# GpSimd makes the weights' low parts in pieces of at most 256 columns in place of 384 to 1280

## What is computed

```
for l in range(2):
    mod, modc = silu(c) @ w_mod[l] + b_mod[l], silu(c_ctx) @ w_mod[l] + b_mod[l]   # 6 x 1024 each
    h, hc = modulated rms_norm of x and xc
    p, pc = h @ w_in[l], hc @ w_in[l]
    y_a = chunked mLSTM (both directions), y_b = latent attention, y_c = neighbourhood attention
    y = (sigmoid(gates) * (y_a, y_b, y_c) summed) @ w_out[l]
    x = x + g1 * y
    x = x + g2 * (square(relu(norm(x) @ w_ff1[l])) @ w_ff2[l])
    # the same for the context stream xc, in the first layer alone
```

## Time and profile before

| what | value |
|---|---|
| median of 3 runs | 1687.56 us (1683.96 to 1689.25) |
| the profiled execution's own time | 1691.04 us |
| its span, first to last instruction | 1689.3 us |
| mean granted clock of PE | 0.97 of full speed |
| PE busy | 93% of the span |
| DVE, ACT, POOL busy | 59%, 45%, 41% |
| PE's share of the chain of waits | 77% |

### The profile page before, as it was taken

How to read it: one execution, slowest core, us unless ns; L and a number is a source line. 1 busy time by engine, 2 the same in 40 slices (tenths; PEclk the granted TensorE clock), 3 DMA queues, 4 the chain that set the end, 5 groups by cost and what they waited for, 6 DMA issues and landing times.

```text
span 1689.3 us, 24992 instructions
## 1 busy us (share of the span) xinstructions
PE 1576.3 (93%) x9728; PEld 1341.6 (79%) x9728; DVE 1000.5 (59%) x1737; ACT 757.5 (45%) x1506; POOL 691.4 (41%) x407
## 2 busy tenths in 40 slices
PE   7897998989999999899999998979898989989998
PEld 3776778967877687688888886967897876889998
DVE  5755934875367762668696964144127287665554
ACT  4424653455544643523232334347436545554443
POOL 0451324634343012455554543534455453234442
PEclk9998999999999999999999998989999999999999
DMA  8442434421225132243455742132520343435553
GB/s 328 185 183 81 181 113 150 151 100 53 83 100 193 26 128 97 75 159 122 169 199 193 279 151 100 69 100 81 162 101 26 122 144 101 157 129 192 179 178 122
DMA packets 69852, 230.64 MB, mean 137 GB/s; under 512 B 18280, under 2 KB 24808, under 8 KB 56424
## 3 DMA queue, kind: packets, MB, share of 16 engines
q1 hardware_dynamic: 60880, 213.67, 35.7%
q10 hardware_dynamic: 8856, 15.39, 2.5%
HBM read 216.45 MB, written 12.58 MB: 136 GB/s over the span
## 4 chain that ended last, share of the span: by engine, by line
PE 77%; DVE 9%; ACT 6%; POOL 4%; issue 3%; DMA 1%; ACTq 0%; DVEq 0%
PE bank L1843 39%; PE bank L1925 10%; PE bank L1881 8%; PE bank L1863 4%; PE bank L1907 3%; PE bank L2228 2%; PE bank L2204 2%; PE bank L2215 2%; POOL wL L693 1%; ACT wH L832 1%; POOL wL L695 1%; PE bank L2078 1%; DVE arena L1339 1%; DVE mjunk L1268 1%; PE bank L1946 1%
## 5 line engine op out<-in xcount | busy, mean ns | idle before, releaser
L695 POOL TENSOR_TENSOR wL<-raw,wH 128x768 fp32r<-128x768 f32 (+3 forms) x198 | 327.7, 1655 | 354.5 <-ACT wH L832 354.4
L832 ACT ACTIVATE wH<-raw 128x768 fp32r<-128x768 f32 (+6 forms) x396 | 296.9, 807 | 387.4 <-PE bank L1843 287.3
L693 POOL TENSOR_TENSOR wL<-raw,wH 128x1280 fp32r<-128x1280 f32 (+2 forms) x144 | 298.8, 2075 | 413.3 <-ACT wH L832 413.3
L1843 PE MATMUL bank<-hH,wH 128*128 128x512 f32 (+1 forms) x720 | 247.8, 344 | 2.4 <-POOL wL L695 1.5
L1843 PE MATMUL bank<-hH,wL 128*128 128x512 f32 (+1 forms) x720 | 244.6, 340 | 0.0
L1843 PE MATMUL bank<-hL,wH 128*128 128x512 f32 (+1 forms) x720 | 244.5, 340 | 0.0
L1843 PE MATMUL bank<-oH,wH 128*128 128x512 f32 (+1 forms) x576 | 194.5, 338 | 0.5 <-issue 0.5
L1843 PE MATMUL bank<-oH,wL 128*128 128x512 f32 (+1 forms) x576 | 193.6, 336 | 0.0
L1843 PE MATMUL bank<-oL,wH 128*128 128x512 f32 (+1 forms) x576 | 193.6, 336 | 0.0
L1271 DVE SCALAR_TENSOR_TENSOR acc<-acc,cb 128x1024 f32<-128x1024 f32 x88 | 167.2, 1914 | 2.5
L1881 PE MATMUL bank<-hH,wH 128*128 128x512 f32 (+1 forms) x384 | 138.8, 362 | 18.0 <-POOL wL L695 11.7
(11 more groups left out here) (213 smaller groups left out, 3140.7 us busy)
## 6 DMA issues: line engine op xcount, KB each, us to landing
raw<-in_p_ff SPq DMA_DIRECT2D x64, 1024.0 KB, 4.8
acc<-in_p_mod SPq DMA_DIRECT2D x44, 1024.0 KB, 5.4
raw<-in_p_ml SPq DMA_DIRECT2D x12, 1024.0 KB, 5.0
raw<-in_p_na SPq DMA_DIRECT2D x12, 1024.0 KB, 4.9
raw<-in_p_mgc SPq DMA_DIRECT2D x16, 512.0 KB, 3.5
raw<-in_p_mga SPq DMA_DIRECT2D x16, 512.0 KB, 3.5
raw<-in_p_mgb SPq DMA_DIRECT2D x16, 512.0 KB, 3.6
raw<-in_p_out SPq DMA_DIRECT2D x8, 1024.0 KB, 4.8
```

The costliest lines, as they stand in the source:

```text
L693: pool.tensor_tensor(l_[:, 0:cut], r_[:, 0:cut], h_[:, 0:cut].bitcast(F32), ALU.subtract)
L695: pool.tensor_tensor(l_[:, cut:k * w], r_[:, cut:k * w], h_[:, cut:k * w].bitcast(F32), ALU.subtract)\
L832: act.activation(flat(wH, n)[:, part], flat(raw, n)[:, part], ACT.Copy)\
L1843: ins = pe.matmul(dst, w_[:, kk, c:c + P], r_[:, kk, lo:TOK], start=kk == k0 and m == 0, stop=kk == k0 + kn - 1 and m == 2)
```

## The change

In `low`, each of POOL's two subtractions is cut into instructions of at most 256 columns. The waits for `w_high` stay where they were, ahead of the first piece of each part, and `w_split` is raised by the last piece. What is computed is the same, and no other engine's list changes.

```diff
-                if not SHARED[n]:
-                    pool.wait_ge(*S("w_high").at(2 * n + 1))
-                    pool.tensor_tensor(l_[:, 0:cut], r_[:, 0:cut], h_[:, 0:cut].bitcast(F32), ALU.subtract)
-                pool.wait_ge(*S("w_high").at(2 * n + 2))
-                pool.tensor_tensor(l_[:, cut:k * w], r_[:, cut:k * w], h_[:, cut:k * w].bitcast(F32), ALU.subtract)\
-                    .then_inc(S("w_split").handle, 1)
+                for part, (lo, hi) in enumerate(((0, cut), (cut, k * w))):
+                    if part or not SHARED[n]:
+                        pool.wait_ge(*S("w_high").at(2 * n + 1 + part))
+                        for at in range(lo, hi, 256):
+                            cols_ = slice(at, min(at + 256, hi))
+                            ins = pool.tensor_tensor(l_[:, cols_], r_[:, cols_], h_[:, cols_].bitcast(F32), ALU.subtract)
+                ins.then_inc(S("w_split").handle, 1)
```

## The result

The changed kernel takes **1700.76 us** (median of 4 runs, 1699.39 to 1704.67), the kernel before 1687.05 in the same comparison: ratio 1.0087, 95% interval 1.0072 to 1.0103, so it is 13.7 us slower (12 to 17). The forecast was 1696 us, slower. The profiled execution took 1700.19 us with a span of 1698.5. The one on record for the kernel before (1691.04) is 4 us over its median; a second one, taken later (experiment e8), took 1688.35, and against that one the changed kernel is 11.84 us late. One execution of experiment e10 took 3371.54 us, twice all others, and is left out of e10's median.

What follows compares the result with a forecast made beforehand. PE was taken to bound the long feed-forward stretches, POOL counting only where PE waits for it. 6.6 + 5.5 - 3.6 = +8.5 us on the median 1687.56 gave 1696 us; own range 1690 to 1702, 8-in-10 range 1686 to 1709.

Steps and rivals of the forecast that it cites:

- Part one: At eleven places of POOL on the chain, 47 more instructions at 0.14 us each: 6.6 us lost.
- Part two: At 66.67, 151.31 and 701.05 us, DVE operations take more turns between POOL's pieces: 2.0, 2.0 and 1.5, sum 5.5 us lost.
- The rival that DVE keeps out: DVE gets no turn between pieces without a wait between them: +8 us, 1695.5 us; chance 0.12.
- The rival that the feed-forward of layer 0 tips over: POOL's blocks there end too late, PE waits in up to 13 at 0.7 us: +9 more, 1705 us; chance 0.14.
- In the feed-forward of layer 0 PE stays without gaps: Sign of the forecast in the profile after: no PE waits there, a block's pieces and three multiplies ending 0.5 us early.
- Part three: PE's waits for DVE at lines 1606 and 1656 shorten, 2 of 7.0 and 1.6 of 4.0 us: 3.6 us gained.
- Behind pieces of 0.69 or 0.42 us the seven take about 5: Step of Part three: DVE's seven operations, 466.21 to 473.63 us before, take about 5 us behind the shorter pieces.
- one per POOL instruction: Claim in Part three: line 1339's four small multiplies, 0.49 us alone, take 4.08 by entering singly behind POOL's instructions.
- two instructions and then free: Step of Part three: PE's longest wait for DVE, 2.2 us, gains almost nothing, as eight instructions will hold DVE instead.

Runs made afterwards that it cites:

- e8: The kernel before, unchanged, run once more for a second profiled execution: median 1686.23 us, profiled execution 1688.35 us.
- e10: The kernel before with pieces of at most 256 columns only for the latent attention weights of layer 0: 1685.17 us, ratio 0.9990.
- e1: The changed kernel with the feed-forward weights of layer 0 split whole again, one instruction per part: 1692.86 us, ratio to before 1.0035.
- e2: The kernel before with the feed-forward weights of layer 0 alone split in pieces of at most 256 columns: 1697.45 us, ratio 1.0061.
- e6: The changed kernel with the two multiplies of every modulation chunk on 128 of their 1024 columns: 1686.67 us, 8.3 us over e5.
- e5: The kernel before with the two multiplies of every modulation chunk on 128 of their 1024 columns: 1678.41 us, ratio 0.9955.

## Why the prediction was right, and where it was off

The sign held, and of the three parts the first two nearly to the size. The total was close because the other errors had opposite signs.

**Part one** (47 x 0.14 = 6.6 lost). The price stands at three sizes: 0.14 at 256 columns, 0.15 more per piece at 128, and at 512 a block of five takes 5.17 for 4.74, 0.14 again. The part had 27 of its 47 instructions between 1055 and 1277 us (three full blocks, one `gate`, one shared, four `ns`), 3.8 us. The same stretch of the program in the base, in the changed kernel and in e1, whose instructions there are those of the changed kernel: its length, then PE's busy time, and the granted clock third from the end.

```profile
1055.00:1277.00 222.00, 195.65 (x1481) 181.78 (x1481) 65.94 (x164) 103.03 (x218) 107.45 (x82) 0.95 0.32 103
```

```profile
1065.60:1292.80 227.20, 197.03 (x1482) 182.48 (x1481) 66.05 (x164) 102.88 (x218) 122.31 (x189) 0.93 0.31 100
```

```profile
1054.70:1285.10 230.40, 200.31 (x1482) 186.00 (x1481) 66.07 (x164) 102.88 (x217) 121.94 (x189) 0.92 0.30 99
```

PE is idle 26.35, 30.17 and 30.09 us: 3.8 and 3.7 more than in the base, as priced. The rest of the 5.2 and 8.4 us is busy time, 1.4 and 4.7 us longer at a lower granted clock. That is also why taking the feed-forward's pieces out (e1) gave back less than they cost alone (e2); what set the clock lower in e1 stays open. So price and count fit this stretch. Which places stand on the chain did change, as in these three `gate` blocks (seven waits at line 1926 for four):

```profile
1158.43 5.82 POOL wL L696 x10
...
1164.60 2.90 POOL wL L696 x5
```

**Part two** (5.5 lost by turns at three places). At the first place 1.98 us measured, 2.0 forecast. At the second POOL's five pieces take 6.82 us for 2.47 + 1.94, +2.41 for 0.42 + 2.0, but PE's wait there grew only from 5.71 to 7.16, 1.45. At the third it grew from 0.99 to 3.16, 2.17 for 0.84 + 1.5. The mechanism was right for operations as long as these: POOL and DVE change turns at the end of a piece, without any wait between. The rival that DVE keeps out falls, since DVE's multiplies of 863.99 to 872.89 each went in between two pieces. The Trainium skill (GPSIMD Engine Reference, section 2.1) has a core of POOL start its next instruction as soon as its own share of the last is done. The prediction concluded from this that no turn would be handed over. The page doesn't say that, and it is the conclusion that the trace refutes: in the earlier trace rows POOL's second instruction starts 0.04 us before the end of the first (1065.94 for 1063.04 + 2.94), as by the page, and turns are handed over all the same.

**The rival that the feed-forward of layer 0 tips over** came half true, and is the largest error: 7.1 us in the trace, 7.9 by e1. The step that failed is "In the feed-forward of layer 0 PE stays without gaps", and behind it the block that the forecast took for all: three multiplies go in between its pieces, and 9.0 us for it was exact. But three blocks tip by 0.5 to 2.5 us, and the fullest has seven entries, five of multiplies and two of the hidden-layer operations; e6 shows that without the long multiplies none does. I had rows of a typical block and none of the fullest one.

**Part three** (3.6 gained) was too small. PE's waits for the two DVE lines fell by 7.5 of 11.0 us in the changed kernel, and the pieces in the attention alone gain 5.4 to 6.8 us net. The step "Behind pieces of 0.69 or 0.42 us the seven take about 5" failed in its size. The seven operations took 7.4 us behind whole blocks, 4.08 of them for the four of the rotation. In the changed kernel they are these:

```profile
469.82 0.29 DVE L1603 TENSOR_TENSOR arena<-arena,ropeg 128x128 f32<-128x128 f32 x1
470.14 0.71 DVE L1336 TENSOR_TENSOR arena<-arena,const 128x128 f32<-128x128 f32 x1
470.78 1.57 DVE L1340 TENSOR_TENSOR arena<-arena,const 128x32 f32<-128x32 f32 x4
472.38 0.43 DVE L1342 TENSOR_TENSOR arena<-arena 128x128 f32<-128x128 f32 x1
```

They take 3.0 us, from 469.82 to 472.81, and the four of the rotation 1.57 where I had allowed 2.5. With pieces 0.7 us and more apart, four operations in 1.57 us can't have gone in one per piece, as the prediction had it: they start at 470.78, 471.42, 471.52 and 472.17, two at a gap. The prediction's "one per POOL instruction" doesn't hold before either: the 4.08 us are three operations held for 1.0 to 1.6 us and one of 0.18 beside them. Part three failed also in reasoning that a wait behind "two instructions and then free" gains nothing: that one, 2.2 us at 494.85, is gone too.

**Left out: the clock.** No term of the sum had it. The section on the hardware gives its rows. Behind each of three waits it costs about 1.5 us, and about as much was saved at one place. Over the whole span PE's busy time grew by only 1.1 us, so other low stretches must have become shorter.

**The number.** 1696.0 against 1700.76: 8.5 forecast, 13.7 measured. The forecast had nothing for the feed-forward (7 to 8 lost, 4.3 of them its three waits), nothing for the clock elsewhere, and 2 to 3 us too little for what the attentions give back. The last covers part of the first two, and that 1700.76 lies in the forecast's own range of 1690 to 1702 is owed to this luck: with the attentions' gain as forecast it would have come out at 1703 to 1704 (an estimate, 1700.76 and 2 to 3). POOL's busy time grew by 167.5 us, not 90, since its instructions now contain waits for DVE's turns; 115 with short multiplies (651.5 to 766.9 from e5 to e6).

## What to carry to other kernels

When two engines take turns by instruction, as POOL and DVE do here where DVE's operation has two SBUF inputs, the length of an instruction sets how long the other one waits, and the number of gaps sets how many long instructions of the other get in. So cut the work of one engine only where the other is on the path (here the latent attention: 0.3 to 0.4% faster), and leave it whole where its own end is what PE waits for and the other has a queue of long work ready (here the feed-forward of layer 0: 10.6 us lost by pieces in that stretch alone). Before trusting that cover, look at the block with the most work of the other engine beside it, not at a typical one.

## What the runs showed of the hardware

**TensorE at its lower level after some waits.** Each row is a window of 3 us: its length, the busy time and count of PE, PEld, DVE, ACT and POOL, then the granted clock (PEclk), the DMA share and GB/s. The changed kernel, around the wait of 2.97 us that ends at 73.22:

```profile
70.00:73.00 3.00, 0.25 (x2) 0.00 (x0) 2.97 (x5) 2.64 (x4) 3.00 (x2) 1.00 0.00 0
73.00:76.00 3.00, 2.78 (x13) 2.78 (x14) 2.90 (x4) 2.28 (x7) 3.00 (x3) 0.52 0.52 156
76.00:79.00 3.00, 3.00 (x25) 3.00 (x25) 2.93 (x3) 0.00 (x0) 3.00 (x3) 0.91 0.97 355
```

A granted clock of 0.52 means nearly the whole window at 1.2 GHz instead of 2.4, and 13 matmuls were done where the kernel before did 27. The lag grows by 2.8 us over the wait, and by 1.4 more until 74 us. The same came after the waits of 3.16 us at 706 (0.84, then 0.60) and of 2.45 us at 875 (0.88, then 0.55). It was saved once: the kernel before had 0.63 in the window 497 to 500, behind its wait of 2.22 us at 494.85, and the changed kernel, without that wait, 1.00.

It isn't a matter of the wait's length alone. With 512 columns everywhere PE waited 2.78 us at 704, longer than the 2.45 us, and lost no clock behind it:

```profile
701.00:704.00 3.00, 0.38 (x2) 0.00 (x0) 2.49 (x3) 2.49 (x4) 3.00 (x3) 1.00 0.00 0
704.00:707.00 3.00, 2.84 (x12) 2.35 (x13) 2.36 (x2) 0.63 (x1) 3.00 (x3) 1.00 0.59 180
```

**The same wait, two lengths of the low clock.** Two executions of the kernel before, in the same window behind the norm at 676 us: first the one on record, then e8.

```profile
682.00:688.00 6.00, 5.96 (x18) 4.23 (x18) 4.83 (x11) 3.90 (x11) 3.90 (x3) 0.65 0.00 0
```

```profile
682.00:688.00 6.00, 6.00 (x24) 4.87 (x24) 6.00 (x13) 4.67 (x12) 1.79 (x3) 0.87 0.00 0
```

18 matmuls and 24: here is the 1.5 us of lag that the execution on record adds between 680 and 700, of the 2.7 by which the two differ. Steps of this size in an otherwise equal program make one pair of profiles an uncertain measure: it gave 9.15 us for a difference of 13.7.
